# Heads of a gated token mixer: the value products, the low parts of the probabilities and the weight splits take other places in the queues

## What is computed

```python
hm = mlstm_chunkwise(q, k, v, i_pre, f_pre)            # per head: num / den
hm = hm * lax.rsqrt(jnp.mean(hm * hm, axis=-1, keepdims=True) + EPS)
hm = o_gate * (hm * mh_norm)
hp = multiscale_pool(proj[..., OFF_P:], pool_w, pool_scale)
x = x + jnp.concatenate([hm, hp], axis=-1) @ w_out
...
scores = (q @ k.T) * dw        # dw: exp of the gates' running sums, causal
num = scores @ v
den = max(abs(sum(scores)), exp(-m))
```

## Time and profile before

| | |
|---|---|
| median of three runs | 919.94 us (919.29 to 921.27) |
| the profiled execution | 921.71 us |
| its span (first to last instruction) | 919.9 us |
| TensorE busy, share of the span | 898.9 us, 98% |
| VectorE, ScalarE, GpSimd busy | 682.9, 456.3, 46.0 us |
| mean granted TensorE clock | 0.992 of full speed |
| read from memory | 89.14 MB, 99 GB/s |

### The profile page before, as it was taken

How to read it: one execution, slowest core, us unless ns; L and a number is a source line. 1 busy time by engine, 2 the same in 40 slices (tenths; PEclk the granted TensorE clock), 3 DMA queues, 4 the chain that set the end, 5 groups by cost and what they waited for, 6 DMA issues and landing times.

```text
span 919.9 us, 15638 instructions
## 1 busy us (share of the span) xinstructions
PE 898.9 (98%) x5598; PEld 810.7 (88%) x5598; DVE 682.9 (74%) x1176; ACT 456.3 (50%) x752; POOL 46.0 (5%) x64
## 2 busy tenths in 40 slices
PE   7999999999999999999989999999999999999995
PEld 6899999999888888888878788999999999888885
DVE  7799999999643434677886679799999998624334
ACT  7556566666432323535762355556666665423220
POOL 0000000000000000001444200000000000000001
PEclk9999999999999999999999999999999999999998
DMA  6233333322432332222211132233333332432312
GB/s 240 69 115 106 101 102 103 113 92 79 161 115 95 110 112 94 85 92 75 63 53 60 56 115 80 93 103 96 109 110 96 103 103 91 138 115 100 106 46 91
DMA packets 38996, 91.73 MB, mean 100 GB/s; under 512 B 4288, under 2 KB 6464, under 8 KB 38960
## 3 DMA queue, kind: packets, MB, share of 16 engines
q1 hardware_dynamic: 38640, 90.72, 30.2%
q0 software_dynamic: 176, 0.46, 0.2%
q10 hardware_dynamic: 144, 0.08, 0.0%
HBM read 89.14 MB, written 2.10 MB: 99 GB/s over the span
## 4 chain that ended last, share of the span: by engine, by line
PE 87%; DVE 7%; ACT 3%; issue 2%; DMA 2%; POOL 0%; DVEq 0%; ACTq 0%; SPq 0%
PE ps L357 15%; PE ps L359 15%; PE ps L358 15%; PE ps L463 13%; PE ps L465 13%; PE ps L464 12%; DVE w_lo L1336 1%; PE ps L387 1%; DMA mask<-consts 1%; PE ps L409 1%; PE ps L390 1%; PE ps L393 1%; DMA raw<-weights 1%; ACT w_hi L782 1%; DVE w_lo L1219 0%
## 5 line engine op out<-in xcount | busy, mean ns | idle before, releaser
L1219 DVE TENSOR_TENSOR w_lo<-raw,w_hi 128x1024 fp32r<-128x1024 f32 x84 | 105.3, 1255 | 123.3 <-ACT w_hi L782 117.6
L357 PE MATMUL ps<-act_hi,w_hi 128*128 128x512 f32 (+1 forms) x470 | 178.8, 380 | 0.2 <-DVE act_lo L1689 0.2
L359 PE MATMUL ps<-act_hi,w_lo 128*128 128x512 f32 (+1 forms) x470 | 178.2, 379 | 0.0
L358 PE MATMUL ps<-act_lo,w_hi 128*128 128x512 f32 (+1 forms) x470 | 178.2, 379 | 0.0
L463 PE MATMUL ps<-xg_hi,w_hi 128*128 128x256 f32 x608 | 174.9, 288 | 1.5 <-DVE work L1372 1.5
L465 PE MATMUL ps<-xg_hi,w_lo 128*128 128x256 f32 x608 | 172.1, 283 | 0.0
L464 PE MATMUL ps<-xg_lo,w_hi 128*128 128x256 f32 x608 | 171.9, 283 | 0.0
L782 ACT ACTIVATE w_hi<-raw 128x1024 fp32r<-128x1024 f32 x76 | 80.2, 1057 | 165.5 <-PE ps L359 163.1
L463 PE MATMUL ps<-xe_hi,w_hi 128*128 128x256 f32 x456 | 128.0, 281 | 0.0
L465 PE MATMUL ps<-xe_hi,w_lo 128*128 128x256 f32 x456 | 127.2, 279 | 0.0
L464 PE MATMUL ps<-xe_lo,w_hi 128*128 128x256 f32 x456 | 127.2, 279 | 0.0
(11 more groups left out here) (205 smaller groups left out, 1410.9 us busy)
## 6 DMA issues: line engine op xcount, KB each, us to landing
raw<-weights SPq DMA_DIRECT2D x85, 512.0 KB, 3.3
raw<-weights SPq DMA_DIRECT2D x152, 256.0 KB, 2.7
x<-x_t SPq DMA_DIRECT2D x8, 256.0 KB, 7.0
first<-weights SPq DMA_DIRECT2D x8, 256.0 KB, 6.7
out<-x SPq DMA_DIRECT2D x6, 256.0 KB, 2.3
out<-x SPq DMA_DIRECT2D x4, 128.0 KB, 2.3
arena<-pool_w POOLq DMA_DIRECT2D x1, 256.0 KB, 3.2
vec<-vecs ACTq DMA_DIRECT2D x1, 73.5 KB, 3.1
```

The source lines that it names most:

```text
L357: pe.matmul(acc, hi, m_hi, start=first, stop=False)
L358: pe.matmul(acc, hi, m_lo, start=False, stop=False)
L359: return pe.matmul(acc, lo, m_hi, start=False, stop=last)
L1219: dve.tensor_tensor(w_lo[:, k % SLOTS], raw[:, k % RAWS], f32(w_hi[:, k % SLOTS]), ALU.subtract).then_inc(lo_made, 1)
```

## The change

In all, the work stays what it was: the same instructions on each engine, in another order.

TensorE: `values(h)` goes ahead of `head_rep(h-1)`, with one more wait (until VectorE has taken in the mean of head h-1, which lies in the same bank); `spread(3)` moves from behind `values(1)` into `proj(2)`, ahead of its step 5; the mean of head 1 comes one step earlier, that of head 2 one later. VectorE: the low part of the probabilities goes ahead of the root's nine steps in each head and behind the intake of the mean (`head_mean_in`, a new function cut from `head_rsqrt`); `head_columns` goes ahead of `mixed` in each head; in the loop each weight split comes one head later, and behind it the splits stand behind the pool steps. ScalarE: `square_num` ahead of `mixed_hi`, `probs_hi` and `copy_r` of the next head behind them, the splits moved alike.

```diff
--- before.py
+++ after.py
@@ -78,7 +78,7 @@
 SUMW = 64
 STEPS = 10
 HSTEPS = STEPS + 3
-MEAN_AT = (4, 5, 5, 3, 4)
+MEAN_AT = (4, 5, 4, 4, 4)
 
 
 
@@ -610,6 +610,7 @@
                         pe.wait_ge(v_made, TB)
                     else:
                         pe.wait_ge(t1_made, h)
+                        pe.wait_ge(hcol_step, HSTEPS * (h - 1) + 4)
                     for S in range(TB):
                         w = T - S * P
                         v = slice(h * P, (h + 1) * P)
@@ -650,6 +651,8 @@
                         if i == 1 and k == 3:
                             values(0)
                             spread(2)
+                        if i == 2 and k == 5:
+                            spread(3)
                         if mean_of is not None and k == MEAN_AT[i]:
                             head_mean(mean_of)
                         if k == 2 and rep_of is not None:
@@ -715,10 +718,8 @@
                     if h == 0:
                         spread(1)
                     else:
+                        values(h)
                         head_rep(h - 1)
-                        values(h)
-                        if h + 2 < HEADS:
-                            spread(h + 2)
                 proj(4, HEADS - 1)
                 proj(5, rep_of=HEADS - 1)
                 proj(6)
@@ -1104,29 +1105,29 @@
                 act.wait_ge(pw_in, 16)
                 act.activation(act_hi[:, PW], arena[:, 4], ACT.Copy).then_inc(pw_hi_made, 1)
                 weights_of(1)
-                for h in range(HEADS):
-                    if h:
-                        if h + 1 < HEADS:
-                            copy_r(h + 1)
-                        probs_hi(h)
-                        if h == 1:
-                            split_next()
-                    else:
-                        square_num(0)
-                    if 1 <= h < HEADS - 1:
+                square_num(0)
+                gate(0)
+                probs_hi(1)
+                copy_r(2)
+                split_next()
+                for h in range(1, HEADS):
+                    if h + 1 < HEADS:
                         weights_of(h + 1)
                     gate(h)
-                    if h:
-                        split_next()
-                        mixed_hi(h - 1)
-                        square_num(h)
-                split_next()
+                    square_num(h)
+                    mixed_hi(h - 1)
+                    if h + 1 < HEADS:
+                        probs_hi(h + 1)
+                    if h + 2 < HEADS:
+                        copy_r(h + 2)
+                    split_next()
                 mixed_hi(HEADS - 1)
                 split_next()
                 pool_hi(0)
                 split_next()
                 pool_hi(1)
                 pool_mixed_hi(0)
+                split_next()
                 pool_hi(2)
                 split_next()
                 pool_mixed_hi(1)
@@ -1641,13 +1642,15 @@
                     dve.scalar_tensor_tensor(t1, ps_num, scalar_of(V_MH + h), gate_of[h % 2],
                                              ALU.mult, ALU.mult).then_inc(t1_made, 1)
 
-                def head_rsqrt(h):
-                    count = HSTEPS * h + 3
+                def head_mean_in(h):
+
                     dve.wait_ge(ms_h, h + 1)
                     dve.scalar_tensor_tensor(acol[:], ps_col[:, SUMW * TB:SUMW * TB + TB], TINY, dcol[:],
                                              ALU.add, ALU.add).then_inc(hcol_step, 1)
-                    dve.wait_ge(hcol_step, count + 1)
-                    rsqrt(hcol_step, count + 1)
+
+                def head_rsqrt(h):
+                    dve.wait_ge(hcol_step, HSTEPS * h + 4)
+                    rsqrt(hcol_step, HSTEPS * h + 4)
 
                 def mixed(h):
                     dve.wait_ge(h_rep, h + 1)
@@ -1700,49 +1703,38 @@
                 split_next()
                 dve.wait_ge(pw_hi_made, 1)
                 dve.tensor_tensor(act_lo[:, PW], arena[:, 4], f32(act_hi[:, PW]), ALU.subtract).then_inc(pw_made, 1)
-                for h in range(HEADS):
-                    if h:
-                        head_product(h - 1)
-
-                        if h % 2 == 1:
-                            head_rsqrt(h - 1)
-                            probs_lo(h)
-                        else:
-                            probs_lo(h)
-                            head_rsqrt(h - 1)
-                    if h == 1:
-                        split_next()
+                gate(0)
+                head_columns(0)
+                probs_of(1)
+                for h in range(1, HEADS):
+                    head_product(h - 1)
+                    head_mean_in(h - 1)
+                    probs_lo(h)
+                    head_rsqrt(h - 1)
                     gate(h)
-                    if h == 0:
-                        head_columns(0)
-                    if h == 1:
-                        mixed(0)
+                    split_next()
                     if h + 1 < HEADS:
                         probs_of(h + 1)
-                    if h == 1:
-                        head_columns(1)
-                    if h >= 2:
-                        mixed(h - 1)
-                    if h:
-                        split_next()
-                        mixed_lo(h - 1)
-                    if h >= 2:
-                        head_columns(h)
+                    head_columns(h)
+                    mixed(h - 1)
+                    mixed_lo(h - 1)
                 head_product(HEADS - 1)
+                head_mean_in(HEADS - 1)
                 head_rsqrt(HEADS - 1)
+                split_next()
                 pool_in(0)
-                split_next()
                 mixed(HEADS - 1)
                 mixed_lo(HEADS - 1)
+                split_next()
                 pool_in(1)
-                split_next()
                 pool_mean(0)
                 pool_lo(0)
+                split_next()
                 pool_in(2)
-                split_next()
                 pool_mean(1)
                 pool_lo(1)
                 pool_mixed_lo(0)
+                split_next()
                 pool_mean(2)
                 pool_lo(2)
                 pool_in(3)
```

## The result

| | before | changed |
|---|---|---|
| median, side by side | 920.61 us (918.08 to 922.51, 6 runs) | 913.65 us (912.12 to 915.39, 6 runs) |
| ratio, 95% interval | | 0.9931, 0.9915 to 0.9948 |
| a second comparison, side by side | 920.13 us (22 runs) | 913.80 us (6 runs), 0.9932, 0.9915 to 0.9949 |
| profiled execution, its span | 921.71, 919.9 us | 913.21, 911.2 us |

The change makes the kernel 0.7% faster, by 6.3 to 7 us.

A forecast was written before the change was run, and what follows sets the result against it. TensorE, busy 898.9 of 919.9 us, bounds the kernel. Won 4.5 + 1.3 + 1.7 = 7.5 us, given back 1.0, so 6.5; the median would be 913.4 or 915.1 us by clock, middle 914.2, range 911.8 to 918.0.

The forecast's parts named there:

- The holes as the sum of the gain: TensorE's five waits in the heads, 4.5 us with restarts, and one at the pool product, 1.3 us, all close.
- The clock term: Slow TensorE steps at low clock behind the longest hole, 478.94 to 484.05 us: a loss of 1.7 us won back.
- What was taken back, 1.0 us: New waiting: 0.2 us for root and low part, 0.4 for head 3's values, 0.4 for the scaled pool output.
- Low part ahead of the root, values ahead of the spread: Heads 1 to 3: head 1's holes of 0.16 and 0.37 us close, values fill head 2's 1.03 us root wait.
- Columns ahead of the mixing, one split fewer: The 1.70 us hole ahead of head 2's mean closes fully, and the 0.41 us ahead of head 1's mean.
- the spread of sums: Head 3's spread of sums moved by six steps on TensorE; exponentials end a little later, costed at nothing.
- The spare time of head 3: Chain from the root's spread to head 3's values: 6.2 us against TensorE's 7.3, spare 0.8 to 1.1 us.
- the slower rival: The values' new wait binds in every head, eating the gain; 924 us at 3 us each plus low clock; chance 0.06.
- the ring: Closed chain across heads of spread, mixing, product, low part, values; decides when it takes over 9.5 us instead of 6.2.
- GpSimd beside the low part: Rival: GpSimd's sum of probabilities holds up head 1's low part, 0.8 us more waiting, 915.0 us; chance 0.14.
- Pool splits: Removing the 1.88 us split ahead of the pool's mean closes the first pool product's hole of 1.3 us.
- The new wait of 0.4 us for the scaled pool output: Behind the heads, TensorE waits for VectorE's scaled pool output, spare 0.75 us; 0.4 us kept, bounds 0 and 1.3.

The follow-up runs named there:

- columns late: Changed kernel with the columns of heads 2 and 3 behind the mixed low part again; 913.51 us, ratio 0.9916.
- head splits early: Changed kernel with the weight splits inside the heads back in their old places; 914.51 us, ratio 0.9931.
- low part twice: Changed kernel with the low part of the probabilities of heads 1 to 3 computed twice; 920.53 us, ratio 0.9991.
- core only: Changed kernel with pool splits, splits inside the heads, and columns of heads 2 and 3 all back in their old places; 919.72 us, ratio 0.9996.
- spread first: Changed kernel with the root's spread ahead of the values on TensorE again; 916.90 us, ratio 0.9949.
- twice in head 3: Changed kernel with the low part of the probabilities computed twice in head 3 alone; 914.32 us, ratio 0.9933.
- only columns: Kernel before with only the columns of heads 2 and 3 moved straight behind the probabilities; 920.07 us, ratio 0.9993.
- only the pool splits moved: Kernel before with only the weight splits behind the heads moved, on VectorE and ScalarE; 919.43 us, ratio 0.9984.

## Why the prediction came out right

**The holes as the sum of the gain.** Right, in kind and in size. Predicted were 4.5 us in the heads and 1.3 us at the pool product, 5.8 us. At full clock, on one chip, the changed kernel is at 909.0 and the one before at 914.9 us: 5.9 us, with an error of about 1 us. The signs that the prediction named all came: no wait for the columns or the root, the values of head 1 straight behind the scores, no low clock from 460 to 500 us, no wait of the first pool product.

**The clock term.** The prediction took half of 1.7 us because it could not know whether the median run has the low clock. On the chip where both ran side by side the means differ by 6.05 us, of which 0.2 are clock (0.9945 and 0.9947). So the term was 0.2 to at most about 1 us (0.9932 against 0.9943 in the other comparisons), not 1.7. The single low stretch of the profiled execution did close, but runs have such stretches elsewhere too, as the 0.66 between 10 and 15 us shows.

**What was taken back, 1.0 us.** Wrong: only 0.05 us of waiting came. These two errors, 1.0 us too much taken back and about 0.65 us too much clock, nearly cancelled; the forecast of 914.2 us was 0.5 us off. That it lay so near is in part luck: it was also reckoned from a median of three runs, 919.94 us, and the six runs that the changed kernel is compared with had 920.61 us. The gain was forecast as 5.7 us and measured as 6.3 to 7.0 us.

**Low part ahead of the root, values ahead of the spread.** Right. Undoing one of them brings 5.6 us of idle time, undoing the other 3.1 us; the change needs both.

**Columns ahead of the mixing, one split fewer.** The hole closed as forecast, the reason was half of it. On the kernel before, columns and square were late by nearly the same: moving the columns alone wins 0.5 of 1.7 us, and with the square ahead too no wait for the mean is left. In the changed kernel either of the two moves of the heading is enough for this hole: it stays closed with the columns late and with the head splits early, and it opens to 2.25 us when both (and the pool splits, which come later in the queues) are taken back.

**What was not tried alone.** ScalarE's new order, the spread of sums for head 3 in its new place and the new places of the means were never taken back in the changed kernel. The prediction put the spread of sums at nothing; no wait in the changed profile speaks against that, but no run prices it.

**The spare time of head 3.** The prediction's chain gave 0.8 to 1.1 us. The profile has none. It let the mixing start when the root's spread ends (470.1 us by its row of 1.1 us from 469.01), but VectorE came to it only at 471.85 us, because split, probabilities and columns stand ahead in its queue, with 0.95 us for a third step of 0.17. What already stood in VectorE's queue was left out. From the mixing on the chain was shorter than reckoned, 4.5 us (471.85 to 476.36) where the prediction's terms make 5.2, because the mixed low part was faster than its mean (0.69 against 1.15 us). So the two errors met at zero spare and no wait. The run with the low part twice shows how the slower rival would begin: 1.4 us of delay in each head, not 2.2, already used up the gain in the median, since lateness adds up along the ring and in that profile the clock fell behind the last wait. It did not make the kernel slower than before.

**GpSimd beside the low part.** The rival of 915.0 us did not come, though both ran at the same time. (Its own terms, 0.5 us and a restart of 0.16, make 0.7 us and not 0.8; and the slower rival's 914.2 + 9 + 1.7 us make 924.9 and not 924. Neither touches the forecast.) GpSimd's and ScalarE's timelines:

```profile
450.62 2.64 POOL L1189 TENSOR_TENSOR key_sum<-key_sum,arena 128x256 f32<-128x256 f32 x2
```

```profile
453.36 1.28 ACT L1057 ACT_TABLE_LOAD   x1 [1.41 <-POOL key_sum L1189]
```

The low part of head 1 took its plain 1.49 us at 450.62 us; GpSimd's two additions, started at the same moment, took 2.64 us instead of 1.31. The exponentials of the next head then waited 1.41 us for that sum, which cost nothing. By the section "SBUF: two separate sides" of the Trainium skill's "SBUF — State Buffer", the one of the two that starts first keeps the shared port pair for its whole instruction and the other is blocked. The trace agrees with one being held for the time of the other: here it was GpSimd, by 1.3 us beside a low part of 1.49 us.

**Pool splits.** The wait closed as forecast. The new wait of 0.4 us for the scaled pool output did not come. How much the move is worth depends on the rest: 1.1 us of idle time on the kernel before, 0.3 us in the changed one.

## What to carry to other kernels

When one engine is the bound and everything else feeds it through strict queues, list its holes with their restarts and add them up; but find the whole set of late things behind each hole, and not only the last, before giving its price to one move. Moves of that kind do not add: three that cost 0.3, 0 and 0.8 us of idle time when taken back alone cost 3.4 us together. Where a chain runs from one iteration into the next, measure its spare time by adding a known delay: lateness is handed on, and when the chain starts is set by what stands in the queue ahead of it.

## What the hardware showed

The size of a hole does not say by itself whether the clock falls behind it. It stayed full behind 1.87 us (spread first, head 1) and 1.43 us (twice in head 3) and even behind 2.25 us in the profile of core only, and fell to half behind 1.20 us (only columns) and behind 1.70 us, the latter both in the kernel before and, for nearly 7 us from 477 us on, with only the pool splits moved. In these three profiles another hole of 1.0 us had ended some 6 us before; whether that matters no run tells. Two windows of the profile with only the pool splits moved:

```profile
478.00:480.00 2.00, 2.00 (x5) 1.54 (x6) 1.66 (x11) 0.00 (x0) 0.00 (x0) 0.50 0.01 4
480.00:482.00 2.00, 2.00 (x6) 1.59 (x5) 1.40 (x1) 0.00 (x0) 0.00 (x0) 0.50 0.00 0
```

The mean clock follows the holes only loosely: the three lowest, 0.9918 to 0.9922, belong to kernels with 3.4 to 5.6 us of idle time, but spread first has 3.1 us and 0.9953, the changed kernel none and 0.9943 and 0.9947. The spread of runs was widest with holes (core only 915.9 to 922.2 us, clock 0.996 to 0.989; changed 912.1 to 915.4 us). What decides it between runs of the same kernel stays open.

A short VectorE step can pay as much beside GpSimd as a long one. The step on 4 columns at 470.86 us above took 0.95 us, 0.8 us more than the 0.17 us that it takes elsewhere, and ended at 471.81 us, just as GpSimd's addition of that time ended (471.79 us). The kernel before has the same pair at 462.22 us, 0.95 us, so it could have been read before. The split of 1024 columns in the earlier trace rows took 0.7 us more than the 1.2 us it takes above. GpSimd in the changed kernel, and VectorE in the kernel before:

```profile
470.77 1.02 POOL L1185 TENSOR_TENSOR key_sum<-arena 128x384 f32<-128x384 f32 x1
```

```profile
462.22 0.95 DVE L1633 TENSOR_TENSOR dcol<-dcol,em 128x4 f32<-128x4 f32 x1
```
